# Nine of eleven feed-forward up chunks with the weights as the stationary operand

## The reference

```python
D_MODEL = 1024
SEQ = 256
D_FF = 2816

def swiglu(x, w_in, w_out):            # layers 0 and 1
    h = x @ w_in                       # (256, 1024) @ (1024, 5632)
    return (jax.nn.silu(h[..., :D_FF]) * h[..., D_FF:]) @ w_out

def swiglu_2(h, w_gate, w_up, w_down): # layers 2 and 3
    return (jax.nn.silu(h @ w_gate) * (h @ w_up)) @ w_down
```

## Time and profile before

| | |
|---|---|
| median of three runs | 1225.51 us |
| the profiled execution, its own time | 1226.42 us |
| span of its instructions | 1224.6 us |
| TensorE matmuls | 1188.2 us busy (97%), 5794 |
| TensorE weight loads | 975.9 us busy (80%), 5794 |
| VectorE | 761.3 us busy (62%) |
| ScalarE | 602.3 us busy (49%) |
| granted TensorE clock, mean | 0.997 |
| read from HBM | 212.17 MB, 174 GB/s |

### The profile page before, as it was taken

The page is one execution under the profiler, slowest core; times in us unless marked ns, Lnnn a source line. Parts: engine busy times, 40 slices in busy tenths (PEclk is TensorE's granted clock), DMA queues, the critical chain, the costliest instruction groups (busy, mean ns, idle before and its releaser), DMA issues.

```text
span 1224.6 us, 16805 instructions
## 1 busy us (share of the span) xinstructions
PE 1188.2 (97%) x5794; PEld 975.9 (80%) x5794; DVE 761.3 (62%) x1049; ACT 602.3 (49%) x916; POOL 37.9 (3%) x69
## 2 busy tenths in 40 slices
PE   6999999999999899999999999999999999999997
PEld 5777888888877788888778788888887878888886
DVE  5488555535896855463767676555455777745541
ACT  5455444425674454452465655444346465644430
POOL 0000000000000100000100110000010001000000
PEclk9999999999999999999999999999999999999999
DMA  8566755744622585564364148556626523766550
GB/s 278 176 193 208 255 172 180 240 129 138 236 92 67 174 284 176 193 231 147 123 203 156 52 148 284 188 173 218 212 82 207 167 92 120 246 202 184 168 163 34
DMA packets 163741, 214.07 MB, mean 175 GB/s; under 512 B 15857, under 2 KB 107705, under 8 KB 163680
## 3 DMA queue, kind: packets, MB, share of 16 engines
q1 hardware_dynamic: 155792, 201.44, 51.5%
q10 hardware_dynamic: 7888, 11.84, 3.0%
HBM read 212.17 MB, written 1.06 MB: 174 GB/s over the span
## 4 chain that ended last, share of the span: by engine, by line
PE 79%; DVE 10%; ACT 3%; DMA 3%; POOL 2%; issue 2%; ACTq 1%; SPq 0%; POOLq 0%; DVEq 0%
PE ps L547 24%; PE ps L549 24%; PE ps L548 24%; DVE w_lo L1393 3%; DVE o_acc L1560 2%; DMA raw<-ev_w_in 2%; PE ps L957 2%; PE ps L834 1%; POOL stat L1871 1%; ACT w_hi L1009 1%; PE ps L650 1%; POOL stat L1873 1%; PE ps L658 1%; DVE x L1432 1%; DVE x L1416 1%
## 5 line engine op out<-in xcount | busy, mean ns | idle before, releaser
L1393 DVE TENSOR_TENSOR w_lo<-raw,w_hi 128x1024 fp32r<-128x1024 f32 x380 | 449.6, 1222 | 131.3 <-ACT w_hi L1009 128.4
L1009 ACT ACTIVATE w_hi<-raw 128x1024 fp32r<-128x1024 f32 x380 | 384.3, 1054 | 138.1 <-PE ps L549 70.0
L547 PE MATMUL ps<-w_hi,a_hi 128*128 128x512 f32 x1040 | 414.5, 399 | 6.2 <-DVE w_lo L1393 2.8
L549 PE MATMUL ps<-w_hi,a_lo 128*128 128x512 f32 x1040 | 407.1, 391 | 0.0
L548 PE MATMUL ps<-w_lo,a_hi 128*128 128x512 f32 x1040 | 406.6, 391 | 0.0
L547 PEld LDWEIGHTS ps<-w_hi,a_hi 128*128 128x128 f32 x1040 | 196.1, 189 | 48.5 <-issue 3.5
L549 PEld LDWEIGHTS ps<-w_hi,a_lo 128*128 128x128 f32 x1040 | 196.0, 188 | 42.1
L548 PEld LDWEIGHTS ps<-w_lo,a_hi 128*128 128x128 f32 x1040 | 196.3, 189 | 38.6
L547 PE MATMUL ps<-w_hi,h_hi 128*128 128x512 f32 x480 | 188.7, 393 | 2.4 <-DVE h_lo L1620 1.2
L549 PE MATMUL ps<-w_hi,h_lo 128*128 128x512 f32 x480 | 187.0, 390 | 0.0
L548 PE MATMUL ps<-w_lo,h_hi 128*128 128x512 f32 x480 | 186.8, 389 | 0.0
(11 more groups left out here) (199 smaller groups left out, 727.7 us busy)
## 6 DMA issues: line engine op xcount, KB each, us to landing
raw<-ffn_w_in SPq DMA_DIRECT2D x176, 256.0 KB, 4.2
raw<-w_in SPq DMA_DIRECT2D x96, 256.0 KB, 3.2
raw<-ffn_w_out SPq DMA_DIRECT2D x88, 256.0 KB, 3.9
raw<-w_gate SPq DMA_DIRECT2D x88, 256.0 KB, 3.8
raw<-w_up SPq DMA_DIRECT2D x88, 256.0 KB, 4.5
raw<-w_down SPq DMA_DIRECT2D x88, 256.0 KB, 4.1
raw<-od_w_in SPq DMA_DIRECT2D x40, 256.0 KB, 2.9
raw<-ev_w_in SPq DMA_DIRECT2D x32, 256.0 KB, 4.9
```

Source lines behind the costliest of these rows:

```text
L547: nc.tensor.matmul(ps[:, bank, :], hi, wh, start=first, stop=False)
L549: return nc.tensor.matmul(ps[:, bank, :], lo, wh, start=False, stop=last)
L1009: nc.scalar.activation(w_hi[:, v.slot, :], raw[:, v.raw, :], ACT.Copy).then_inc(w_high, 1)
L1393: V.tensor_tensor(w_lo[:, v.slot, :], raw[:, v.raw, :], w_hi[:, v.slot, :].bitcast(F32), ALU.subtract).then_inc(w_low, 1)
```

## The change

The new functions are `column_unit` and `column_chunk` on TensorE, `silu_columns` and `split_columns` on ScalarE, `glu_columns` and `split_columns` on VectorE. Chunks 2 to 10 swap the operands: a 128x128 block of weights is stationary and the 256 tokens are moving. The result stands in PSUM with hidden features on the partitions: one bank holds the gate half (two blocks of 128 features, 256 tokens each), the other the up half. Silu and product work on 128x512 at once, and the split reads `glu` in SBUF. Chunks 0 and 1 stay as they were. The turn of chunk 0 stays in its place, and that of chunk 1 moves to where the turn of chunk 10 was, in `down`; therefore `down` takes the feature blocks 2 and 3 as numbers 14 and 15 (`D_ORDER`). The number, size and timing rule of the weight transfers stay; only the down rows come in the other order.

```diff
-        FFN_BUF = (0, 1, 0)
+        D_ORDER = (0, 1, *range(4, KF - KD + 2), 2, 3, *range(KF - KD + 2, KF))
...
+            def column_unit(v, q, banks):
+
+                for i in range(2):
+                    k = 2 * q + i
+                    for h in range(2):
+                        for b in range(2):
+                            o, col = ps[:, banks[h], SEQ * b:SEQ * (b + 1)], CH * i + FC * h + P * b
+                            wh, wl = w_hi[:, v.slot, col:col + P], w_lo[:, v.slot, col:col + P]
+                            nc.tensor.matmul(o, wh, a_hi[:, k, :], start=(k == 0 and b == 0), stop=False)
+                            nc.tensor.matmul(o, wh, a_lo[:, k, :], start=False, stop=False)
+                            mm = nc.tensor.matmul(o, wl, a_hi[:, k, :], start=False, stop=(k == KD - 1 and b == 1))
+                            if (k, h, b) == (KD - 1, 0, 1):
+                                mm.then_inc(acc_done, 1)
+                return mm
+
+            def column_chunk(l, units, c, banks):
+
+                pe.wait_ge(glu_done, c + (NC + 2) * l)
+                for q, v in enumerate(units):
+                    pe.wait_ge(w_low, v.n + 1)
+                    column_unit(v, q, banks).then_inc(w_used, 1)
...
-                pe.wait_ge(glu_done, glu_at(l, NC - 2, 1))
-                for k in range(joint):
-                    if k == 2:
-                        turn_ffn(l, NC - 1, FFN_BUF[(NC - 1) % LOOP])
+                pe.wait_ge(glu_done, glu_at(l, NC - 2))
+                for i in range(joint):
+                    if i == 2:
+                        turn_ffn(l, 1)
+                    k = D_ORDER[i]
...
                 with pe.Fori(0, (NC - 2) // LOOP) as j:
                     for r in range(LOOP):
-                        units = [Unit(U_C[l] + 4 * (2 + r) + q, j) for q in range(4)]
-                        before = FFN_BUF[(1 + r) % LOOP]
-                        joint_chunk(units, j * LOOP + (2 + r), FFN_BANK[(2 + r) % LOOP], free_ffn,
-                                    lambda c, q: turn_ffn(l, j * LOOP + (1 + r), before) if q == 1 else None)
+                        column_chunk(l, [Unit(U_C[l] + 4 * (2 + r) + q, j) for q in range(4)], j * LOOP + (2 + r),
+                                     FFN_BANK[(2 + r) % LOOP])
...
+            def silu_columns(l, c, r):
+                act.wait_ge(acc_done, c + acc_at(l, "C"))
+                act.wait_ge(glu_done, c + ((NC + 2) * l + 2))
+                nc.scalar.activation(silu[:, 0, :, :], ps[:, FFN_BANK[r][0], :].rearrange("p (b n) -> p b n", b=2),
+                                     ACT.Silu).then_inc(silu_done, 1)
...
+            def split_columns(l, c):
+                act.wait_ge(glu_done, glu_at(l, c))
                 dst = h_hi[:, :, :].rearrange("p (c b) n -> p c b n", b=2)[:, c, :, :]
-                nc.scalar.activation(dst, blocks(0), ACT.Copy).then_inc(h_high.sem, 1)
+                nc.scalar.activation(dst, glu[:, 0, :, :], ACT.Copy).then_inc(h_high.sem, 1)
...
+            def glu_columns(l, c, r):
+                dve.wait_ge(silu_done, glu_at(l, c))
+                dve.wait_ge(w_used, c * 4 + (U_C[l] + 4))
+                dve.wait_ge(h_low.sem, c + (h_low.at(l, 0) - 2))
+                V.tensor_tensor(glu[:, 0, :, :], silu[:, 0, :, :], ps[:, FFN_BANK[r][1], :].rearrange("p (b n) -> p b n", b=2),
                                 ALU.mult).then_inc(glu_done, 1)
```

More of the change, by code:

```diff
@@ L313, in out_at, with glu_at, split_at @@
             return 2 * sum(NA[:l]) + (2 * t + c if c < 2 else 2 * c + t) + 1
-        def glu_at(l, c, t):
+        def glu_at(l, c, t=0):
+            return (NC + 2) * l + 2 * t + c + 1 if isinstance(c, int) and c < 2 else c + ((NC + 2) * l + 3)
+        def split_at(st, l, c):
             if isinstance(c, int) and c < 2:
-                return 2 * NC * l + 2 * t + c + 1
-            return c * 2 + (2 * NC * l + t + 1)
+                return st.at(l, 0 if c == 0 else NC - 1)
+            return c + (st.at(l, 0) - 1)
         NB = 2 * len(LAYERS)
@@ L344, in blocks_kernel @@
         silu_done, glu_done = sem("silu_done"), sem("glu_done")
-        h_turned, h_high, h_low = stage("h_turned", NC), stage("h_high", NC), stage("h_low", NC)
+        h_turned, h_high, h_low = stage("h_turned", 2), stage("h_high", NC), stage("h_low", NC)
         bounds = list(range(NB))
@@ L530, in _ @@
                 wd = w_down(l).rearrange("(k p) n -> k p n", p=P)
-                for k in range(KF):
-                    load(Unit(U_D[l] + k), wd[k, :, 0:CH], wd[k, :, CH:D], False)
+                for i, k in enumerate(D_ORDER):
+                    load(Unit(U_D[l] + i), wd[k, :, 0:CH], wd[k, :, CH:D], False)
             for t in range(NT):
@@ L946, in turn_y, with turn_ffn @@
                     turn_tile(y_part(l, first + t)[2], src[:, t, :], y_turned)
[L949 removed]
+            def turn_ffn(l, c):
                 pe.wait_ge(glu_done, glu_at(l, c, 1))
[L952 to L954 removed]
                 for b in range(2):
@@ L957, in turn_ffn @@
                         tr = nc.tensor.transpose(tb[:, 0, SEQ * b + P * t:SEQ * b + P * (t + 1)],
-                                                 glu[:, buf, t, P * b:P * (b + 1)], ident)
+                                                 glu[:, c, t, P * b:P * (b + 1)], ident)
                 tr.then_inc(h_turned.sem, 1)
@@ L1372, in _ @@
                         c = j * LOOP + (2 + r)
-                        ffn_split(l, j * LOOP + (1 + r))
-                        for t in range(NT):
-                            silu_part(l, c, (2 + r) % LOOP, t)
+                        silu_columns(l, c, (2 + r) % LOOP)
                         for q in range(4):
                             high(Unit(U_C[l] + 4 * (2 + r) + N_W + q, j))
+                            if q == 1:
+                                split_columns(l, c)
                 fed[0] += 4 * (NC - 2)
-                ffn_split(l, NC - 1)
+                ffn_split(l, 1)
                 feed(U_D[l] + KF - KD + N_W)
@@ L1851, in _ @@
                     for r in range(LOOP):
-                        ffn_split(l, j * LOOP + (1 + r))
-                        for t in range(NT):
-                            glu_part(l, j * LOOP + (2 + r), (2 + r) % LOOP, t)
+                        c = j * LOOP + (2 + r)
+                        glu_columns(l, c, (2 + r) % LOOP)
                         for q in range(4):
                             low(Unit(U_C[l] + 4 * (2 + r) + N_W + q, j))
+                            if q == 1:
+                                split_columns(l, c)
                 fed[0] += 4 * (NC - 2)
-                ffn_split(l, NC - 1)
+                ffn_split(l, 1)
                 feed(U_D[l] + KF - KD + N_W)
```

61 lines of the change are left out of this document (29 added, 32 removed).

## The result

In nine runs of each on the chip the changed kernel took 1233.3 us in the median (1230.51 to 1234.62), the kernel before 1228.87 us (1224.09 to 1232.09). The ratio is 1.0042, with a 95% interval of 1.0024 to 1.0060: slower, by about 5 us. The forecast was 1220.6 us and 4.9 us faster, with a range up to 1231.

The account below looks back on a forecast made before the run. TensorE's own stream was taken to bound the feed-forward stage. Added matmul time of 10.9 us less 15.8 us of removed turns gave -4.9 us, so 1225.51 became 1220.6 us, range 1210 to 1231.

Parts of the forecast that it names:

- the new waits: In loop and `down`: ScalarE's split waits about 1 us for VectorE's product, covered by the ring of twelve slots; cost 0.
- the four packets: Instruction queue q8: some 4 packets more, as the four loop bodies grow; 8 or more would speak for refetching.
- rival C: Feed-forward loops: the larger body's instructions are fetched again, +4 us (1229) or, with three packets per branch, 1247; chance 0.08.
- The turn removed: Feed-forward loops on TensorE: 36 turns of four transposes leave, 0.44 us each, 15.8 us in all.
- the pace of the added matmuls: Loop on TensorE: matmuls of 256 columns take 0.1170 us each, two costing 0.2340 against 0.2277 for one of 512.
- The added part: Loop on TensorE: 24 matmuls of 256 columns replace 12 of 512 in each of 144 units, 10.9 us more.
- The break-even of 0.1184: Loop on TensorE: at 0.1184 us per matmul of 256 columns (11.37 / 96) the gain is nil.
- rival B: Loop on TensorE: weight loads become the bound from a pace of 0.1184; at 0.120, +5.5 us, 1231; chance 0.17.
- the upper bound by rows 5: Loop on TensorE: the wider printed distance, 0.12, gives 11.52 us per chunk, +5.5 us.
- The two printed distances: TensorE's starts around one full load beside 256 columns, 0.11 to 0.12 apart, taken to show that such a load hides.
- Rival A: Loop on TensorE: the fixed part shrinks with the column count, pace near 0.1135, -17 us, 1208.6; chance 0.10.

Follow-up runs that it names:

- e7: The kernel before, but a turn in its loop transposes one block of four; 1216.16 us beside 1226.99.
- e1: The changed kernel, but the three chunks of a loop pass take 64, 128 and 192 of the 256 tokens as moving columns, with full loads; 1429.55 us.
- e5: The changed kernel, but the three chunks of a loop pass take 208, 224 and 240 of the 256 tokens as moving columns, with full loads; 1204.06 us.
- e2: The changed kernel, but the three chunks of a loop pass load 32, 64 and 96 of the 128 stationary columns, all 256 tokens moving; 1216.49 us.
- e6: The changed kernel, but the three chunks of a loop pass load 80, 112 and 120 of the 128 stationary columns, all 256 tokens moving; 1216.33 us.
- e10: The changed kernel, but every column matmul in its loop starts a new sum, so none adds onto what stands in PSUM; 1233.01 us.
- e3: The kernel before, activations stationary and turns kept, but each loop matmul of 512 columns is cut into two of 256; 1249.99 us beside 1227.3.

## Why the prediction was wrong

**The frame held.** TensorE's stream is the path of the stage, nothing waits in it before or after, ScalarE's and VectorE's changes cost nothing, the new waits are hidden, the instruction count and the four packets came as said, and the loop body is not fetched again (rival C). The turn removed was worth its 0.44 us: e7 confirms 0.11 per transpose. Removed: 15.8 us, as forecast.

**The term that was mis-sized** is the pace of the added matmuls: "I take 0.1170, between them and at the rows of the same operand and width, since loads alone are faster than that." It is 0.1200, and 3456 matmuls make 10.4 us of the 3 ns. The added part is 15.8 + 5.5 = 21.3 us, not 10.9, and -4.9 becomes +5.5. The break-even of 0.1184 follows from the rows, and rival B, "the loads become the bound", gave +5.5 us at 0.120, the upper bound by rows 5; it had a chance of 0.17.

**The step that failed** is the reason behind it. The full load sets 0.112 (e1, e5), 256 columns can follow each other at 0.1133 with other loads (e2, e6), and the sum took the larger of two paces, with 0.117 for the latter. But 256 columns with a full load each take 0.120, more than either. The rows at 0.117 had narrow loads; they were no measurement of the disputed case, and what looked like a bare pace was not the lowest one. The rows ahead of the prediction held a better estimate: a matmul of 512 columns with a full load takes 0.2267, of which 512 / 2.4 GHz = 0.2133 is its own length, and the 0.0133 left over, put on the 0.1067 of 256 columns, gives 0.1200, an estimate that hits what was measured. The prediction saw that each matmul has a fixed part, but read its size from the rows with narrow loads. That the 0.0133 holds at any width is not shown either (0.0115 to 0.0117 at 244 to 252 columns). The two printed distances with one full load (0.12 and 0.11) were single events after narrow ones, and carried no steady stream. Rival A's 0.1135 is met with loads of 64, 80 and 112 columns, not with the full load of this kernel. Rival B's name was half right: the loads do not set the pace alone, since at 240 moving columns it is 0.1117.

**The range** failed by a second thing. The forecast was set on the median of three runs, 1225.51. Nine runs of the same kernel had 1228.87. With that base, +5.5 gives 1234.4 (measured 1233.3), above the 1231 where the range ended; it had reserved nothing for the base.

**What stays open**: why a full load makes a matmul of 256 columns take 6.7 ns more than a load of 112 does. It isn't the adding in PSUM (e10) nor which operand is stationary (e3). The loads' unevenness (0.1133 at 112 columns, 0.1159 at 96, 0.1177 at 32) may be a matter of how load and matmul fall in time, but no run shows that, and a narrower result is not excluded for them.

## What to carry to other kernels

When a change exchanges few wide matmuls for twice as many narrow ones, the columns stay and the loads double; the pace must be measured with loads of the real size in a steady stream, since two things that each fit can take more time together than the longer one. Where no such stream is in the trace, a first estimate is to take the part of a matmul beyond its columns from rows with the same load, even at another width: here it would have been exact at 256 columns and 1.7 ns too much at 244 to 252. A margin of 1.4 ns (0.1170 to 0.1184) decided this change; where a sum of large terms of both signs hangs on such a number, the two signs deserve nearly equal chances. And if the weights are to be stationary, the moving operand should be made wide by other means (here by putting the high and low parts side by side).

## What the runs showed of the hardware

- A stream of fp32r matmuls with a full 128x128 load each: 0.112 us per matmul at 64 and from 192 to 240 moving columns, then 0.1132 (244), 0.1150 (248), 0.1167 (252), 0.1200 (256), and 0.227 at 512. From 240 to 252 each column adds its own length alone; over the columns' length there are 11.5 to 11.7 ns at 244 to 252 and 13.3 ns at 256 and at 512.
- 256 moving columns with a load of 64, 80 or 112 columns: 0.1133 to 0.1135; with 32, 96 or 120: 0.1159 to 0.1177 (e2_load, e6_load_2).
- In e1_moving, with 64, 128 and 192 moving columns, TensorE was busy throughout, and yet the granted clock fell to the lower level, 1.2 GHz: 0.50 in the window of 128 columns, after a chunk of 64. In all twelve loop passes of the trace it fell during the chunk of 64 columns and came back during that of 192. A matmul with a full load then took 20.52 / 96 = 0.214, nearly twice the 0.112 at the higher level: the load-paced stream slows down with the clock. The kernel took 1429.55 us with less work. In the windows of e5_moving_2 (208 to 240 columns) it stayed at 1.00.
- Two stretches of 4 and 5 us at a clock of 0.57 and 0.66, worth some 3 us, stood in one profile and not in the other. A difference of two profiled spans can't be read more finely than that; the windows over one loop can.
